# Even layer: the first scores of a pair of heads between the two full groups of the gate projection

## What is computed

```
z = u_lat @ w_in
...
s_win = einsum("bqhd,brqjhd->bhqrj", q_r, k_win) + bias
s_ctx = einsum("bqhd,bkhd->bhqk", q_r, k_ctx)
p = softmax(concatenate([s_win, s_ctx]))
...
y_b = attention(q, k, v, k_c, v_c, rpb) * silu(z[..., OFF_BG:E_IN])
y_lat = concatenate([y_a, y_b], axis=-1) @ w_out
```

## Time and profile before

| | |
|---|---|
| median of 3 runs | 2447.63 us (2441.5, 2447.63, 2447.99) |
| the profiled execution | 2441.66 us, of which the span is 2439.8 us |
| PE busy | 2270.2 us, 93% of the span |
| DVE, ACT, POOL busy | 1501.9 us, 1189.5 us, 514.2 us |
| mean granted TensorE clock | 0.972 |
| the even layer's 8 rounds | from about 118 us to about 1294 us of the span |

### The profile page before, as it was taken

One profiled execution on the slowest core, in us unless ns is written; L12 is line 12 of the kernel. 1 busy time (PEld: TensorE's weight loads), 2 busy tenths in 40 slices (PEclk: granted clock), 3 DMA queues, 4 the chain that ended last, 5 costly groups with the idle time before them and its releaser, 6 DMA issues. The chain is left out here.

```text
span 2439.8 us, 34401 instructions
## 1 busy us (share of the span) xinstructions
PE 2270.2 (93%) x12000; PEld 1975.0 (81%) x12000; DVE 1501.9 (62%) x2368; ACT 1189.5 (49%) x1714; POOL 514.2 (21%) x303
## 2 busy tenths in 40 slices
PE   4799999999999999999997999799999999995998
PEld 3688888888888888888875888688898889884887
DVE  5176575765757657576586346566775685576534
ACT  4244434445344453434444234276686577667422
POOL 1423232332313223132221100112111211210300
PEclk7899999999999999999998999899999999997999
DMA  6211111211121111111107555101111111113744
GB/s 244 61 50 60 55 55 52 73 49 55 56 74 51 49 63 56 65 51 49 54 26 267 155 160 164 41 27 69 52 43 43 52 69 43 43 52 125 227 152 142
DMA packets 165346, 199.70 MB, mean 82 GB/s; under 512 B 51064, under 2 KB 125944, under 8 KB 162168
## 3 DMA queue, kind: packets, MB, share of 16 engines
q1 hardware_dynamic: 155304, 174.53, 22.1%
q10 hardware_dynamic: 9792, 23.07, 2.7%
q0 software_dynamic: 144, 0.52, 0.1%
HBM read 166.11 MB, written 31.98 MB: 81 GB/s over the span
## 5 line engine op out<-in xcount | busy, mean ns | idle before, releaser
L950 PE MATMUL ps<-u_hi,w_hi 128*128 128x512 f32 (+1 forms) x1536 | 559.4, 364 | 16.6 <-POOL w_lo L637 16.6
L950 PE MATMUL ps<-u_hi,w_lo 128*128 128x512 f32 (+1 forms) x1536 | 544.8, 355 | 0.0
L950 PE MATMUL ps<-u_lo,w_hi 128*128 128x512 f32 (+1 forms) x1536 | 543.9, 354 | 0.0
L950 PEld LDWEIGHTS ps<-u_hi,w_hi 128*128 128x128 f32 x1536 | 290.4, 189 | 53.6 <-POOL w_lo L637 16.7
L950 PEld LDWEIGHTS ps<-u_hi,w_lo 128*128 128x128 f32 x1536 | 290.2, 189 | 41.9
L950 PEld LDWEIGHTS ps<-u_lo,w_hi 128*128 128x128 f32 x1536 | 291.0, 189 | 37.2
L1524 POOL TENSOR_TENSOR o_w_lo<-o_w_raw,o_w_hi 128x1024 fp32r<-128x1024 f32 x48 | 124.7, 2599 | 715.4 <-ACT o_w_hi L1539 715.4
L1784 PE MATMUL ps<-u_hi,o_w_hi 128*128 128x426 f32 (+2 forms) x640 | 238.3, 372 | 14.0 <-POOL o_w_lo L1524 9.3
L742 ACT ACTIVATE probs<-probs,neg_max 128x640 f32<-128x640 f32 (+1 forms) x160 | 122.8, 768 | 251.8 <-DVE neg_max L858 250.7
L637 POOL TENSOR_TENSOR w_lo<-w_stage,w_hi 128x1024 fp32r<-128x1024 f32 x64 | 153.3, 2395 | 425.5 <-ACT w_hi L695 425.5
L1784 PE MATMUL ps<-u_hi,o_w_lo 128*128 128x426 f32 (+2 forms) x640 | 237.5, 371 | 0.0
(11 more groups left out here) (176 smaller groups left out, 4287.8 us busy)
## 6 DMA issues: line engine op xcount, KB each, us to landing
y_tile<-y_scratch SPq DMA_DIRECT2D x72, 512.0 KB, 5.0
w_stage<-in_w_even SPq DMA_DIRECT2D x64, 512.0 KB, 3.3
o_w_raw<-in_w_odd SPq DMA_DIRECT2D x48, 512.0 KB, 3.3
ada_piece<-in_w_ada SPq DMA_DIRECT2D x16, 1024.0 KB, 5.2
wout_raw<-in_w_out SPq DMA_DIRECT2D x16, 1024.0 KB, 9.9
ada_pieces<-in_w_ada SPq DMA_DIRECT2D x4, 2048.0 KB, 18.3
y_scratch<-h_backward SPq DMA_DIRECT2D x16, 512.0 KB, 2.7
h_scratch<-h_tile ACTq DMA_DIRECT2D x18, 256.0 KB, 2.3
```

The lines of the kernel that those rows point to most:

```text
L950: last = nc.tensor.matmul(ps[:, bank(j, g), 0:t - f], w[:, slot, c * P:(c + 1) * P], x[:, c, f:t], start=(c == 0 and n == 0), stop=(c == K ...
```

## The change

On PE alone, the four matmuls of `scores(i, 0)` stand before group 1 of the gate projection and no longer behind it. No instruction is added or removed, and no wait is written differently.

```diff
@@ def body(i, last), of PE in even_layer
                 turn_v(i)
                 project(i, BG, 0)
+                scores(i, 0)
                 project(i, BG, 1)
-                scores(i, 0)
                 project(i, BG, 2)
                 for s in range(STEPS):
```

## The result

The changed kernel takes 2483.15 us (median of 4 runs, 2479.17 to 2485.2), the kernel before 2447.4 us (median of 4). The ratio is 1.015, 95% interval 1.0132 to 1.0167: slower, by some 36 us. Forecast were 2481 us, range 2466 to 2494, chance of slower 0.96. The profiled execution of the changed kernel took 2485.20 us, 43.5 us more than that of before (2441.66 us).

What follows compares the result with a forecast made beforehand. PE was taken to set the pace in the changed rounds; 22.6 us of net wait plus 15 us of slower clock made 38 us, giving 2479 from the profiled execution or 2485 from the median, so 2481 us, range 2466 to 2494.

Steps and rivals of the forecast that it cites:

- The wait: PE before the moved first scores: stands still until the second v remainder is made, 4.25 us a round with the release.
- The old waits as a credit: PE's waits for step 0's row maximum and softmax, before the second scores and transposes: 1.43 us a round, gone.
- Net wait: Each of 8 even-layer rounds: new wait 4.25 less old waits 1.43 is 2.82 us, 22.6 us in all.
- The clock: PE behind the new wait: granted clock falls in each of 8 rounds, 1.9 us each, 15 us in all.
- the upper bound of 2.5 us: Most that one fall of PE's clock costs a round, from the odd layer's long fall: 12 matmuls lost.
- Copies of step 0: DVE's copies after the transposes: about 1 us later relative to PE, fits in 3.8 us of cover, costed at nothing.
- two sums, 2479 and 2485: The 38 us loss added to the profiled execution's 2441.66 us, or to the timed runs' median 2447.63 us.
- The rival "no change": First scores or later in the round: moved wait hidden or delay taken up by slack, 2442 to 2448 us; chance 0.03.
- "faster": First scores between groups 0 and 1: wait under the 1.43 us it removes, 2430 at no wait; chance 0.01.

Runs made afterwards that it cites:

- experiment 3: Changed kernel, but the first scores stand after 4 of the 8 chunks of gate group 1 (12 matmuls): 2447.86 us, ratio 1.0006 to the kernel before.
- experiment 4: Kernel before, TensorE order kept; v roundings on ScalarE and v remainders on VectorE put ahead of gate group 0's tanh and product: 2433.2 us, ratio 0.9949.
- experiment 1: Changed kernel with 18 matmuls that nobody reads put ahead of the first scores in each round: 2467.31 us, ratio 1.0088 to the kernel before.
- experiment 6: Changed kernel's TensorE order, with v roundings and remainders also put ahead of gate group 0's tanh and product: 2444.85 us, ratio 1.0004 to the kernel before.
- experiment 5: Kernel before, order kept, with only a wait for the same four v remainders added behind gate group 0: 2485.14 us, ratio 1.017.
- experiment 2: Changed kernel, but the first scores stand after 2 of the 8 chunks of gate group 1 (6 matmuls): 2467.5 us, ratio 1.0089 to the kernel before.
- experiment 7: Changed kernel with 9 matmuls of no use put ahead of the first scores in each round: 2468.73 us, ratio 1.0094 to the kernel before.

## Why the prediction was right

- *The wait.* Forecast were 4.25 us a round from the end of group 0's issue, measured 286.83 - 282.60 = 4.23 us in the second round, and the idle time is the same 4.0 to 4.1 us in all eight. The chain of tanh, two v roundings and two v remainders was read from the rows of before, and it ran the same with PE at rest.
- *The old waits as a credit.* 1.43 us a round: shown from both sides, by experiment 3 (1.35 us of new wait a round for nothing) and by experiment 4, where the waits are gone and nothing takes their place (8 x 1.43 = 11.4 us of the 12.8 us won; most of the rest is the shorter transposes).
- *Net wait*, 22.6 us forecast: 21.3 us by the medians with the clock kept up behind the scores, and 2.7 to 2.8 us a round in seven rounds of eight against the forecast 2.82 (experiment 1).
- *The clock*, 15 us forecast from the odd layer's seven waits: 15 us by the ratios of the changed kernel and experiment 1, and 40.0 - 22.6 = 17.4 us in the profiled execution, which had five long falls and three short ones. A fall came in each round, as taken, and not in six of seven. A short one cost 4.2 - 2.8 = 1.4 us, a long one 2.4 to 2.8 us; the upper bound of 2.5 us was a little low. The 1.9 us a round were a choice between the two lengths; measured were 17.4 / 8 = 2.2 us.
- *Copies of step 0* cost nothing: in the changed kernel L984 waits for 11.7 us in all, before for 14.3 us.
- *Luck in the last two microseconds.* 2481 lay between two sums, 2479 and 2485, that start from different times of the kernel before. The loss is the better test: 38 us forecast, 36 us measured.
- *What the forecast left out*: the odd layer isn't quite a constant, though the forecast called it unchanged. The same waits with more and longer falls gave 4 us more in this execution. The runs of the kernel before spread over 2439.7 to 2449.5 us, and such falls may be why. Of the 15 runs beside the first four experiments, the seven under 2445 us had a mean clock of 0.969 to 0.973, the eight above it 0.967 to 0.969. That fits, but nothing was tried.
- The rival "no change" was drawn too narrowly: it asked for the whole wait to be hidden, some 4 us sooner, while by the credit in the same sum a wait of 1.43 us is already no change. Experiments 3 and 6 show that, with 1.35 us of wait a round on average and no change in time. In the changed kernel itself the wait stayed at 4.1 us, so both this rival and "faster" fell.

## What to carry to other kernels

An instruction moved ahead of a unit of work on the busiest engine must not wait for that engine's latest result through other engines: here the tanh of group 0 stood ahead of the v roundings in ScalarE's list, so the moved scores waited for the very unit that they followed. Look at what stands ahead of the releaser on its own engine; here that reordering was the gain (12.8 us), and the move the loss. Count a wait that stands later on the same path, and that the new wait would cover, as a credit before costing the new one, and add the clock when the new pause is long: it took two fifths of the loss.

## What the runs showed of the hardware

How often the granted clock fell behind a pause of PE in the even layer went by the pause's length more steeply than the sum assumed. Pauses by the waits' rows, falls by the 10 us stretches:

| pause before the scores or group 1 | falls | kernel |
|---|---|---|
| 4.1 us | 16 of 16 | changed kernel, experiment 5 |
| 2.7 us | 6 of 8, all short | experiment 2 |
| 2.0 us | 1 of 8 | experiment 7 |
| 1.4 us | 0 of 8 | experiment 3 |

The odd layer's seven pauses, the longest 3.5 us, were followed by a fall in six of seven cases in the kernel before, in all seven in the changed kernel, and in 61 of 63 over the nine profiled executions. Length alone does not decide: single pauses of 1.8 us (experiments 1 and 2) and of 2.1 us (experiment 6) were followed by a fall, while most of 2.0 us were not. What else decides was not tried.

The clock's part of the loss is a matter of TensorE not working, not of the delay itself: the same delay filled with matmuls that nobody reads kept 1.00 behind the scores in all eight rounds and was 15 us faster than standing still.
